# State-space input powers in turned layout through DRAM scratch, in a two-layer decoder trunk

## The reference, cut to what matters

```python
lam_dt = lam * jnp.exp(log_dt)[:, None]
lam_bar = jnp.exp(lam_dt)
b_bar = ((lam_bar - 1.0) / lam)[:, :, None] * lax.complex(b_re, b_im)      # (group, state 64, channel 16)
...
bu = jnp.einsum('gph,btgh->btgp', b_bar, u)
s  = scan(s_t = lam_bar * s_(t-1) + bu_t)
y  = jnp.einsum('ghp,btgp->btgh', c, s).real + d_skip * u
z  = gelu(y); val, gate = split(z @ w_out); return val * sigmoid(gate)
```

## Time and profile before

| | |
|---|---|
| median of 3 runs | 1003.06 us |
| span of the profiled execution | 999.6 us |
| PE busy | 987.1 us (99%) |
| DVE busy | 744.5 us (74%) |
| ACT busy | 571.2 us (57%) |
| POOL busy | 114.4 us (11%) |
| DMA, mean | 173 GB/s |

### The profile page before, as it was taken

The page is one execution under the profiler, slowest core; times in us unless marked ns, Lnnn a source line. Parts: engine busy times, 40 slices in busy tenths (PEclk is TensorE's granted clock), DMA queues, the critical chain, the costliest instruction groups (busy, mean ns, idle before and its releaser), DMA issues.

```text
span 999.6 us, 19015 instructions
## 1 busy us (share of the span) xinstructions
PE 987.1 (99%) x7304; PEld 904.0 (90%) x7304; DVE 744.5 (74%) x922; ACT 571.2 (57%) x794; POOL 114.4 (11%) x144
## 2 busy tenths in 40 slices
PE   8999999999999999999999999999999999999997
PEld 8999999989999888888898888888899898888886
DVE  5789986889976777777687777776566587666666
ACT  7444447573365655555465555555599765555555
POOL 4854138100001000000010000001000010000000
PEclk9999999999999999999999999999999999999999
DMA  7555555443075565666646666566544256655563
GB/s 253 192 174 183 170 177 164 149 132 121 23 218 184 183 196 185 190 183 191 196 148 214 189 188 190 184 180 193 186 126 125 85 154 218 190 192 188 190 190 108
DMA packets 49049, 172.57 MB, mean 173 GB/s; under 512 B 6097, under 2 KB 6097, under 8 KB 48977
## 3 DMA queue, kind: packets, MB, share of 16 engines
q1 hardware_dynamic: 48544, 170.99, 54.3%
q10 hardware_dynamic: 432, 0.55, 0.2%
HBM read 170.47 MB, written 1.05 MB: 172 GB/s over the span
## 4 chain that ended last, share of the span: by engine, by line
PE 73%; DVE 13%; POOL 6%; ACT 4%; issue 4%; DMA 1%; SPq 0%; DVEq 0%; POOLq 0%; ACTq 0%
PE mx L1314 11%; PE gu L1314 11%; PE mx L1317 6%; PE gu L1317 6%; PE acc L1356 4%; PE gu L1299 4%; PE gu L1300 4%; PE gu L1301 4%; DVE w_lo L803 4%; PE acc L1360 2%; PE gu L1356 2%; PE mx L1356 2%; PE acc L1343 2%; PE acc L1345 2%; PE acc L1347 2%
## 5 line engine op out<-in xcount | busy, mean ns | idle before, releaser
L803 DVE TENSOR_TENSOR w_lo<-raw,w_hi 128x1024 fp32r<-128x1024 f32 x258 | 324.3, 1266 | 91.0 <-ACT w_hi L364 90.4
L364 ACT ACTIVATE w_hi<-raw 128x1024 fp32r<-128x1024 f32 x259 | 270.5, 1052 | 80.8 <-DMA raw<-wstream_dram 22.3
L1299 PE MATMUL gu<-g,w_hi 128*128 128x256 f32 x560 | 161.4, 288 | 1.5 <-DVE g L943 1.3
L1300 PE MATMUL gu<-g,w_hi 128*128 128x256 f32 x560 | 158.4, 283 | 0.0
L1301 PE MATMUL gu<-g,w_lo 128*128 128x256 f32 x560 | 158.4, 283 | 0.0
L1314 PE MATMUL mx<-g,w_hi 128*128 128x512 f32 x480 | 119.9, 392 | 0.0
L1314 PE MATMUL gu<-g,w_hi 128*128 128x512 f32 x464 | 116.2, 392 | 0.0
L1299 PEld LDWEIGHTS gu<-g,w_hi 128*128 128x128 f32 x560 | 107.3, 192 | 2.3 <-issue 1.5
L1300 PEld LDWEIGHTS gu<-g,w_hi 128*128 128x128 f32 x560 | 107.4, 192 | 0.1
L1301 PEld LDWEIGHTS gu<-g,w_lo 128*128 128x128 f32 x560 | 107.3, 192 | 0.0
L1314 PEld LDWEIGHTS mx<-g,w_hi 128*128 128x128 f32 x480 | 87.0, 189 | 16.0
(11 more groups left out here) (309 smaller groups left out, 1927.1 us busy)
## 6 DMA issues: line engine op xcount, KB each, us to landing
raw<-wstream_dram SPq DMA_DIRECT2D x318, 512.0 KB, 3.7
x<-x_in_dram SPq DMA_DIRECT2D x4, 256.0 KB, 5.9
raw<-wstream_dram SPq DMA_DIRECT2D x3, 256.0 KB, 5.7
out_dram<-x_tok SPq DMA_DIRECT2D x3, 256.0 KB, 2.0
gain_row<-last_gain_dram SPq DMA_DIRECT2D x1, 512.0 KB, 4.4
raw<-wstream_dram ACTq DMA_DIRECT2D x1, 256.0 KB, 4.6
s_memory<-b_re_dram SPq DMA_DIRECT2D x1, 256.0 KB, 4.6
s_memory<-b_im_dram SPq DMA_DIRECT2D x1, 256.0 KB, 5.2
```

What stands on the lines that cost most here:

```text
L364: act.activation(weights(unit)[0], raw[:, s_raw, :], ACT.Copy).then_inc(hi_ready, 1)
L803: dve.tensor_tensor(lo, raw[:, n % RAW, :], hi.bitcast(F32), ALU.subtract).then_inc(lo_ready, 1)
L1299: pe.matmul(dst, a, hi, start=start, stop=False, skip_group_check=check)
L1300: pe.matmul(dst, a, lo, start=False, stop=False, skip_group_check=check)
```

## The change: what it does, and the diff

The powers of the decay for b (4 steps x real and imaginary x 32 pairs = 256 rows of 128 states) are turned by 2 transposes in turn 5 instead of the 64 transposes of finished products. ACT copies them to `powers_rows`. SP stores them to a DRAM scratch (4 DMAs, after the load of unit 24), waits for these stores after the load of unit 25, and reads them back in 16 DMAs, each of which writes one row of 2048 numbers into 16 partitions, two after each of the loads 25 to 32. The turned b comes as a new input `b_turned` (laid out on the host) in 8 DMAs of 256 KB into 32 partitions each, after every second load from unit 9 to 23. DVE multiplies the two in 6 pieces of [128, 2048] in turns 9 to 14 (`in_product`); the six pieces for c move to turns 3 to 8 (`out_product`). ACT writes the products into `state_in` with a mask as scale (8 `pad_in`, two in each of turns 12, 13, 18, 19). POOL gets new pieces: `s5_negate` ahead of `s5_powers`, `s5_mask`, `s5_now` (6 operations of [128, 512]) and `s5_pad_now`, and loses two of its four `s5_pad`. Its clearing of `toep` moves behind `in_padded` and its angle powers move ahead of it. SP's loads 6 to 32 are written out; its loop starts at unit 33.

```diff
 SP:
+            def store_powers():
+                sp.wait_ge(powers_copied, 1)
+                for k in range(2):
+                    for g2 in range(2):
+                        sp.dma_start(powers_dram[g2, 2 * k:2 * k + 2].rearrange("j r a p -> (j r a) p"),
+                                     powers_rows[:, P * k + STATE * g2:P * k + STATE * (g2 + 1)]).then_inc(
+                            powers_stored, 16)
+            def read_powers(r, j):
+                if r == 0 and j == 0:
+                    sp.wait_ge(powers_stored, 16 * 4)
+                for g2 in range(2):
+                    first = CH * j + GROUP * g2
+                    sp.dma_start(powers_t[r][first:first + GROUP, :],
+                                 powers_dram[g2, j, r:r + 1].rearrange("r a p -> r (a p)").broadcast_to(
+                                     [GROUP, PAIRS * STATE])).then_inc(powers_loaded, 16)
+            def read_inputs(r, j):
+                sp.dma_start(in_t[r][CH * j:CH * (j + 1), :], b_turned[r]).then_inc(inputs_loaded, 16)
+            for unit in range(2 * RAW, RAW * spread):
+                load(unit, slot(RAW, unit), unit - RAW + 1)
+                if unit in INPUTS_READ:                      # 9, 11, ... 23
+                    read_inputs(*divmod(INPUTS_READ.index(unit), STEPS))
+                if unit == POWERS_STORED:                    # 24
+                    store_powers()
+                if unit in POWERS_READ:                      # 25 .. 32
+                    read_powers(*divmod(POWERS_READ.index(unit), STEPS))
 ACT:
-            def read_turned(k):
-                act.wait_ge(turned, k + 1)
-                act.activation(*turned_state(k), ACT.Copy).then_inc(turned_read, 1)
+            def read_powers():
+                act.wait_ge(powers_turned, 1)
+                act.activation(powers_rows, mx[:, 0, 0:2 * P], ACT.Copy).then_inc(powers_copied, 1)
+            def pad_in(k):
+                r, g2, half = k // 4, k // 2 % 2, k % 2
...
+                act.activation(state_in[r][:, pairs, STATE * g2:STATE * (g2 + 1)], src[:, pairs, :], ACT.Copy,
+                               scale=group_mask[:, g2:g2 + 1]).then_inc(in_padded, 1)
 DVE:
+            def in_product(k):
+                real, imag = (d.rearrange("p a j h -> p (a j h)") for d in dense)
+                if k == 0:
+                    dve.wait_ge(inputs_loaded, 16 * 2 * STEPS)
+                    dve.wait_ge(powers_loaded, 16 * 2 * STEPS)
+                    dve.tensor_tensor(real, powers_t[0], in_t[0], ALU.mult)
+                elif k == 1:
+                    dve.wait_ge(powers_loaded, 16 * 4 * STEPS)
+                    dve.wait_ge(padded, 4)
+                    step(dve.tensor_tensor(imag, powers_t[1], in_t[1], ALU.mult))
...
 PE:
-            def turn(k):
...
-                for a in range(4):
-                    mm = pe.transpose(mx[:, k % 2, P * a:P * (a + 1)], b_pow[:, k // 8, 4 * (k % 8) + a, :],
-                                      ident[:, :])
-                mm.then_inc(turned, 1)
+            def turn_powers():
+                pe.wait_ge(const_ready, 1)
+                pe.wait_ge(powers_ready, 1)
+                for k in range(2):
+                    mm = pe.transpose(mx[:, 0, P * k:P * (k + 1)],
+                                      powers[:, 0, 2 * k:2 * k + 2].rearrange("p j r a -> p (j r a)"), ident[:, :])
+                mm.then_inc(powers_turned, 1)
 POOL:
+            def s5_now():
+                times = lambda dst, r, i: step(pool.tensor_tensor(
+                    dst, b_raw[:, r], powers[:, 0, STEPS - 1, i, :].unsqueeze(2).broadcast_to([P, PAIRS, GROUP]),
+                    ALU.mult))
+                times(in_dense[:, 0], 0, 0)
+                times(in_tmp[:, 0], 1, 1)
+                step(pool.tensor_tensor(in_dense[:, 0], in_dense[:, 0], in_tmp[:, 0], ALU.subtract))
...
             step(pool.memset(c_zero, 0.0))
+            s5_negate()
             s5_powers()
-            step(pool.memset(b_pow, 0.0))
+            step(pool.memset(state_out, 0.0))
             s5_pad(0)
-            step(pool.memset(state_out, 0.0))
+            s5_mask()
             s5_skip()
-            for i in range(1, 4):
-                s5_pad(i)
+            s5_now()
+            s5_pad(1)
+            s5_pad_now()
+            s5_angle_powers()
+            pool.wait_ge(in_padded, 4)
             pool.memset(toep, 0.0).then_inc(zeroed, 1)
-            s5_angle_powers()
             pool.wait_ge(zeroed, 1)
             s5_tables()
```

More of the change, by code:

```diff
@@ L60 @@
 STEP_ARRAYS, S5_ARRAYS = 4, 5
+POWERS_TURNED, POWERS_STORED, POWERS_READ, INPUTS_READ = 5, 24, range(25, 33), range(9, 25, 2)
+PAD_TURNS = (12, 13, 18, 19)
 GROUP, STATE = 16, 64
@@ L147, in trunk @@
         state_out = arena[:, 8192:16384].rearrange("p (r a s) -> p r a s", r=2, a=PAIRS)
-        b_pow = arena[:, 16384:24576].rearrange("p (r a s) -> p r a s", r=2, a=PAIRS)
+        in_t = [arena[:, 16384 + 2048 * r:18432 + 2048 * r] for r in range(2)]
+        powers_t = [arena[:, 20480 + 2048 * r:22528 + 2048 * r] for r in range(2)]
+        powers_rows = low[:, 0:256]
+        in_now = arena[:, 0:2048].rearrange("p (r a c) -> p r a c", r=2, a=PAIRS)
+        in_dense = arena[:, 2816:3840].rearrange("p (r a h) -> p r a h", r=2, a=PAIRS)
+        in_tmp = low[:, 512:1536].rearrange("p (k a h) -> p k a h", k=2, a=PAIRS)
+        mask_tmp = low[:, 1536:1664]
         c_zero = arena[:, 24576:26624].rearrange("p (r a s) -> p r a s", r=2, a=PAIRS)
@@ L568, in prep_turn @@
                 split_after(g0)
[L569 to L573, removed]
+                if f == POWERS_TURNED:
+                    read_powers()
+                if f in PAD_TURNS:
+                    pad_in(2 * PAD_TURNS.index(f))
+                if f == DECAY_TURN:
                     act.wait_ge(rot_started, 1)
@@ L583, in prep_turn @@
                     read_kernels(f - KERNEL_TURN - 1, range(2, 3))
[L584 to L587, removed]
+                if f in PAD_TURNS:
+                    pad_in(2 * PAD_TURNS.index(f) + 1)
                 split_after(g0 + 2)
@@ L1586, in prep_turn @@
                 column_unit(gu[:, f % 2, 0:SEQ], g0 % RING)
[L1587 to L1590, removed]
+                if f == POWERS_TURNED:
+                    turn_powers()
                 if f == KERNEL_TURN + 1:
@@ new lines, in s5_mask @@
+            def s5_mask():
+                add = lambda dst, a, b_: step(pool.tensor_tensor(dst, a, b_, ALU.add))
+                t = mask_tmp
+                add(t[:, 0:64], ident[:, 0:64], ident[:, 64:128])
+                add(t[:, 64:96], t[:, 0:32], t[:, 32:64])
+                src = t[:, 64:96].rearrange("p (g h) -> p g h", g=2)
+                at = 0
+                for n in (8, 4, 2):
+                    dst = t[:, at:at + 2 * n].rearrange("p (g h) -> p g h", g=2)
+                    add(dst, src[:, :, 0:n], src[:, :, n:2 * n])
+                    src, at = dst, at + 2 * n
+                pool.tensor_tensor(group_mask[:, :].unsqueeze(2), src[:, :, 0:1], src[:, :, 1:2],
+                                   ALU.add).then_inc(mask_ready, 1)
@@ L2037, in s5_pad, with s5_pad_now @@
+            def s5_pad_now():
+                step(pool.memset(arena[:, 0:2048], 0.0))
+                for r in range(2):
+                    halves(lambda rows, cols: step(pool.tensor_copy(in_now[rows, r, :, cols], in_dense[rows, r])))
+                pool.sem_inc(in_now_ready, 1)
+            def s5_pad(r):
+                pool.wait_ge(dense_ready, r + 1)
+                dst = state_out.rearrange("p r a (j c) -> p r a j c", j=STEPS)
                 for g2 in range(2):
                     rows, cols = slice(STATE * g2, STATE * (g2 + 1)), slice(GROUP * g2, GROUP * (g2 + 1))
-                    pool.tensor_copy(dst[rows, i % 2, :, :, cols], dense[i % 2][rows]).then_inc(padded, 1)
```

118 lines of the change are left out of this document (68 added, 50 removed).

## The result

| | before | after |
|---|---|---|
| median of 6 runs, us | 1001.66 (1001.39 to 1003.19) | 1009.7 (1008.08 to 1012.66) |
| ratio, 95% interval | | 1.008 [1.007, 1.009] |
| span of the profiled execution, us | 999.6 | 1007.0 |
| mean granted clock of TensorE in it | 0.999 | 0.995 |

The change costs 8 us. The forecast was 1006.3 with a range of 1001.2 to 1011.0: the sign and the place were right, the size was under half of what came: +3.2 us forecast, +7.4 us in the span.

A forecast was written before the change was run, and what follows sets the result against it. PE is busy 99% of the span, but DVE and POOL were taken to set the pace. 4.6 - 1.1 - 0.3 = +3.2 us: span 1002.8, plus 3.5 to the median, 1006.3 us, range 1001.2 to 1011.

The forecast's parts named there:

- D - 2.24: PE's shift by turn 11: DVE's lateness D, 6.8 us, less 2.24 us spare at turn 9's hidden row, giving +4.6.
- PE's own part: PE's stream in the first feed-forward block: 6.9 us of transposes removed, 0.3 us added in turn 5.
- this shift stays until the kernels are made: Turns 11 to 16 have no transposes before or after, so PE's shift of +4.6 us was to stay unchanged.
- (a) The negation: Ahead of POOL's powers, before DVE's first product: DVE 2.3 us later, with 0.4 us back from its old place.
- (b) s5_now: Six POOL operations beside turns 7 and 8, 7.7 us at a share of 0.44: DVE 3.4 us later.
- (c) The small operations: `s5_mask` 0.4, `s5_pad_now` 1.0 and the moved angle powers 0.1: DVE 1.5 us later.
- SP and the DMAs: Reads and stores in the weight queue: 2.5 us a unit, under 2.88, loads up to 0.8 later; costed 0.
- Rival 3: Narrow 16-partition reads bound turns 8 to 11: +11 us, about +3 if a read costs half; chance 0.14.
- cheaper half: Rival 3's case in which a read costs half as much: about +3 us, under the forecast's delay.
- The second half: Tables in POOL start once the kernels are done, 1.1 us better; DVE's last split 0.3 earlier without an ACT copy.
- Rivals 1 and 2: Rival 1: the gain arrives, D below 1.6, chance 0.12. Rival 2: no difference, D 1.6 to 5.6, chance 0.22.

The follow-up runs named there:

- the run that gives 996.49: Changed kernel with rotation tables early, without the 24 reads and with `s5_now` replaced by one clearing: 996.49 us, ratio 0.9939.
- neither: Changed kernel without the 24 reads and with `s5_now`'s six operations left out: 1001.21 us, ratio 0.9991.
- no reads: Changed kernel without the 8 input and 16 scratch reads, `s5_now` and the stores kept: 1006.55 us, ratio 1.0044.
- `s5_now` cleared: Changed kernel with the six operations of `s5_now` replaced by one clearing of `in_dense`, reads kept: 1008.49 us, ratio 1.0058.
- the pair of runs: Changed kernel without the 24 reads, once with `s5_now` whole (1006.55 us), once without its six operations (1001.21 us).
- wide reads of other data: Changed kernel with the 16 scratch reads replaced by 128-partition reads of the same bytes from the weights: 1008.37 us, ratio 1.0057.
- wide reads of the true data: Tables-early kernel (1005.19 us) with every read back covering 128 partitions, computing the same: 1008.45 us, ratio 1.0054.
- the reads in gaps: Changed kernel with the same 24 reads put in pairs behind every third load: 1010.1 us, ratio 1.0078.
- `s5_now` late: Changed kernel with `s5_now` and `s5_pad_now` moved behind the angle powers and DVE's scaling of turn 12: 1012.75 us, ratio 1.0099.
- all edits together: Changed kernel with reads in pairs behind every third load, `s5_now` behind turn 12's scaling, tables and mask early: 1006.06 us, ratio 1.0044.

## Why the prediction was right in sign and short in size

*The frame held.* PE's shift was to be D - 2.24, with D the lateness of DVE up to the hidden row of turn 9. That row is done at 109.06 instead of 101.70, so D = 7.36, where 6.8 was forecast; PE's shift should be 5.1, and turn 11 is late by 5.25, where 4.6 was forecast. PE's own part (6.6 us less work) agrees with the run that gives 996.49. Two things failed: the terms of D, and the step "this shift stays until the kernels are made", for turn 12 is late by 7.42. The terms can be had from the runs, by the same row: 103.38 with neither, 107.69 with no reads, 109.06 after.

| lateness of turn 9's hidden row, us | forecast | measured |
|---|---|---|
| negation and small operations | 3.4 | 1.68 |
| `s5_now` | 3.4 | 4.31 |
| reads | 0 | 1.37 |

That the sum came within 0.6 us is luck: too much in the first line covers what is missing in the other two. The lines hold in this order only: with `s5_now` cleared and the reads kept, the row is done at 109.16, no earlier than in the kernel after.

*(a) The negation, 2.3 less 0.4: too much.* It took 2.11 us, as expected, but the powers ended at 41.09, not later than before (41.22). The last twelve operations of the chain took 7.5 us instead of 10.5. The first product started at 42.14, not near 43.6, and then only because DVE stood 1.06 and 1.02 us for ACT. I had treated POOL's chain as fixed; it is stretched by DVE just as DVE is by it, and DVE now stood beside it. That is the reading; no run took the negation away by itself. With the reads gone the first product waits for the powers and is 0.60 to 0.73 us late: that much of this term is there, hidden in the kernel after by the reads.

*(b) s5_now, 3.4: 4.05 in the kernel, 4.43 by the pair of runs.* The share of POOL's time, 0.44 from the pad and skip rows, was measured as 0.45. The length was short: 9.9 us for 7.7, since three of the six are stretched to 1.9 to 2.15 us. The Trainium skill's rule (SBUF — State Buffer, Who interferes with whom), that two such instructions exclude each other for their whole length, fits rows of both engines growing at once; taken to its end, 7.7, it overstates the price. Some of POOL's time falls beside DVE's waits and its read of PSUM, about 1 us here; the rest of the difference is not explained.

*(c) The small operations, 1.5: about 1.0 up to turn 9 (1.68 with neither, less the 0.73 of the first product).*

*SP and the DMAs, costed 0: this is the step that failed.* DVE's turn 8 begins 2.37 us late after (82.01 for 79.64) and 1.01 late without the reads (80.65), so the reads add 1.36 us by then. In turn 10, behind the forecast's last row, DVE loses 2.35 us more, by waits of 0.78 and 1.50 for ACT that are not there without the reads; they come out as PE's wait in turn 11, and the shift grows from 5.25 to 7.42. I worked out that the bytes fit, 2.5 us a unit under 2.88, and that DVE, being late, would not see a load that is 0.8 us late. Both halves were wrong. The rate, from the queue's row of before, from 28 to 110 us:

```profile
q1 hardware_dynamic: 4028, 14.65, 55.4%
```

14.65 MB in 55.4% of 82 us are 322 GB/s of engine time; after, the engines were busy 81.1% of 82, 66.5 us; the 25 loads (13.1 MB) at the old rate take 40.7 and leave 25.8 for the 4.2 MB of reads and stores, some 160 GB/s, an estimate, and half the rate I used. From 80 to 90 us the engines were busy throughout (1.00). And a load starts only when its slot comes free, so its landing, 5.4 us where the earlier trace rows have 4.5, counts in full in each unit that ACT needs at once.

*Rival 3* put this at +11 us, or about +3 if a read costs half as much, and gave ACT's waits for `raw` as its sign. The sign came (12.6 us). Its cheaper half was so a true cause beside the forecast's, not a rival to it. Its mechanism, the 16 partitions, is not shown: the run with wide reads of other data gave 1.3 us, which is not clear of noise, and the one with wide reads of the true data was slower. The Trainium skill (SBUF — State Buffer, Door 1: The DMA port swizzle) would have 4 of 16 ports reached. That 128 KB land in 5.8 us narrow and 3.7 wide agrees with the direction, but the source differs too.

*The clock: not foreseen.* In 80 to 100 us the granted clock was 0.91: about 1.8 us of PE's speed. The sum nearly closes: waits 7.9 + clock 1.8 - transposes 3.1 gives 6.6 of the 7.4.

*The second half, -1.4: -0.1.* The tables start right after the last kernel, as said (168.69, 6.4 later with PE 7.4 late: 1.0 gained, 1.1 forecast), but take 16.5 us instead of 15.6, which takes the gain back; the 0.3 us of the ACT copy did not come (the last hidden row is late by 7.34, like the rotation). PE stands 4.17 us before it, forecast about 3.4. What I left unsaid is that this wait could be removed: 4.5 us, by letting the tables start 18 us earlier.

*Rivals 1 and 2* needed D under 5.6. They are out.

*The number.* 1006.3 came from the forecast span, 1002.8, and 3.5 us between span and median. But each run's span lies 1.7 to 2.0 us under its own time (1007.0 and 1008.82 after). The rest of the 3.5 came from the runs: the span of 999.6 fits the fastest of the three, 1001.39, and their median of 1003.06 fell to 1001.66 with three more. With 1.8 the same working gives 1004.6, and a range up to 1009.3, under the 1009.7 measured. That the time lies inside the range is in part luck.

## What to carry to other kernels

When PE is 99% busy, work taken from it is worth only what the engine behind it has spare, so price what the change adds to that engine, the waits that it inherits among them: a read put into the queue of the weights made the loads land later (5.4 us for 4.4 from 28 to 110 us), also before 80 us, where the DMA engines were not full (5.4 for 4.3 at 76.4% busy). Two delays in the same turns hide each other: measure each with the other taken away, or each will look cheap (1.2 and 3.1 us here, 8.5 together). And look for a wait that the change makes needless: here the tables' scratch, not the transposes, was worth 4.5 us.

## What the runs showed of the hardware

After PE stood for 2 us or more, the granted clock often fell in the same or the next stretch of 10 us, though not always. In the kernel with `s5_now` cleared a wait of 4.05 us ends at 100.3, and the stretch from there has 0.70; with the reads in gaps a wait of 3.93 us, to 101.35, was followed by 0.69. PE's stretches with `s5_now` cleared:

```profile
90.00:100.00 10.00, 6.25 (x53) 0.95 0.88 204
100.00:110.00 10.00, 9.70 (x60) 0.70 0.92 202
```

0.70 over 10 us is a loss of 3 us, nearly as much as the wait itself: 60 matmuls, where a full stretch has 86. With `s5_now` late a wait of 3.77 us at 99.3 was followed by 0.83, and with all edits together one of 3.36 us at 70.1 by no loss:

```profile
60.00:70.00 10.00, 6.74 (x57) 1.00 0.48 148
70.00:80.00 10.00, 9.03 (x73) 1.00 0.81 200
```

These stretches are a mix of TensorE's two levels, 1.2 and 2.4 GHz. Which waits bring the lower one can't be told from these runs.
